# The routing ahead of a mixture of experts: the first expert turn's rows by products with one-hot matrices, its table later

## The chip, the cores and the metric

The kernel runs on one core of one Trainium2 chip. The metric is the device time in microseconds (us), as a median over runs. Everything is computed in float32.

## The reference

Two blocks of a model work on 512 tokens of 1024 features. The change is in the last stage of the second block, a mixture of experts. Cut to it:

```
group  = argmax of 4 group logits per token          # one group of 8 experts
top2   = the two best of the group's 8 expert logits # 1024 (token, choice) pairs
h      = rmsnorm(x) * gain + shift
y      = for each pair: silu(h @ w_gate[e]) * (h @ w_up[e]) @ w_down[e]
out    = rmsnorm(x + gate * (w1 * y1 + w2 * y2))
```

There are 32 experts; each has three matrices, 1024 x 512, 1024 x 512 and 512 x 1024, in float32 (2 MB each).

## The kernel before

The stage runs in 16 *turns*, and each turn works on two experts, 2n and 2n+1, with 64 row places each (`SUBROWS`): 128 rows in all. An expert with more than 64 rows gets further places in extra turns, which run only where they are wanted (`over_turns`). Ahead of the turns, `w_o_part` adds the output projection to x and makes the router's logits, and `route_part` does the routing:

- PE turns x to token-major form, in eight halves of four transposes (`turn_x(i)` in `route_part`, L3653). ACT scales each half to a row half in `tok_rows` (L3684) and puts the plain copy back in x (L3687). SP stores the four row tiles to `h_rows` in DRAM (L3638).
- DVE finds group and experts in some 20 small operations. `X` is the one-hot of each of the two choices over 32 experts, `M` their sum (L3750). Products of M with a triangular matrix and with ones give each row's *rank* within its expert (L3660, L3662).
- From rank, expert and the count of over-full experts DVE works out a slot, then the turn and the position in it (L3756 to L3774), then `numbers` (L3776) and the one-hot `one_pos` (L3780). Eight products on PE (L3668) turn these into `table`: which token and which pair stand in each place of each turn. Eight more products (L3673) give the weights of the last turn's rows.
- POOL gathers the rows of a turn from `h_rows` by `table` (L3901), and stores a turn's results to `y_rows` (L3938). A blank scatter (L4097) is sent ahead of the first.

Then the turns. PE transposes the gathered rows (`turn_x(pe, n)`, L3947); ACT (and for turn 0 DVE, L4017) applies gain and shift (L4008); PE multiplies by `w_gate` and `w_upe` (`both_experts`, L3959); ACT takes silu (L4023), DVE multiplies (L4030), PE transposes (L3979), DVE copies (L4036), PE multiplies by `w_downe` (L3959 too) and DVE scales the rows (L4042). The down product of turn n-1 stands on PE after the turn of x for n+1.

The weights come through nine slots of 2 MB. SP sends slots 0 to 7 early, slot 8 after the row stores. `send_quarters` then refills slots 0 to 7 in quarters of 512 KB (L3873): a quarter waits until two of the eight steps of the first or second turn's product have used it. From load 17 on, whole slots are sent (L3852), the first when the down product of turn 0 is done. Before the first quarter stands

```
            sp.wait_ge(gathered[0], 16)
```

Each engine runs its instructions in the order in which they are written; semaphores order the engines. The order is written out by hand: `route.tensor`, `route.vector` and so on, then the loop over turns.

Of the kernel before, what the change touches and what calls it, by code (L numbers as in the profile page):

```python
# [3592 lines left out]
Routing = collections.namedtuple("Routing", "sync gpsimd tensor scalar vector slot_weight_mm counted")  # L3593


def route_part(k, out, x, r_root, experts, weights, table, h_dram, work, at_rows, gather, y_blank, last_token, slot_weight):

# [4 lines left out]
    off = [work]  # L3602

    def buf(*dims):
        n = int(np.prod(dims))
        off[0] += n
        assert off[0] <= 6144
        x = k.at(off[0] - n, n)
# [5 lines left out]
    L, tie, one_g, ex, pg = buf(4, 36), buf(4, 8), buf(4, 4), buf(4, 4), buf(4, 1)  # L3614
    top = [buf(4, 1), buf(4, 1)]
    gmax, least, total = buf(4, 1), buf(4, 1), buf(4, 1)
    picked, masked, part = buf(4, 8), buf(4, 8), buf(4, 4, 8)
    one_e = [buf(4, 8), buf(4, 8)]
    M = buf(4, 32)
    chain, upto = buf(33), buf(33)  # L3620
    own, place, over_n, expert, slot, turn, pos, weight_in = (buf(8) for _ in range(8))
    of_over, over_from, of_turn, one_turn = buf(8, 7), buf(32), buf(8, N_COLS + 1), buf(8, N_COLS)
    one_pos = k.at(at_rows + D, D).rearrange("p (q n) -> p q n", q=8)
    X, chosen = (k.at(at_rows + a, 256).rearrange("p (i a n) -> p i a n", i=2, a=4) for a in (0, 256))
    numbers = k.at(at_rows + 512, 16 * N_COLS).rearrange("p (q t n) -> p q t n", q=8, t=2)
    of_count = k.at(40960, 224).rearrange("p (n t) -> p n t", n=32)
    late = k.at(4096, (OVER + 1) * 32).rearrange("p (o n) -> p o n", o=OVER + 1)
    halves_of_x = [x[:, 4 * (i % 2):4 * (i % 2) + 4, P * (i // 2):P * (i // 2) + P] for i in range(8)]
    x_banks = (0, 2, 3, 5)
    tok_rows = [k.at(D * tt, D) for tt in range(4)]  # L3630
    s = {n: k.sem("route_" + n) for n in ("step", "exped", "rank_in", "rank", "table_in", "table_mm", "table", "rows", "rows_out", "x_turned", "x_rows",
                                         "last_token", "weight_in", "slot_weight_mm", "counted")}
# [697 lines left out]
```

## Time and profile before

| | |
|---|---|
| median of 3 runs | 1899.35 us (1894.31 to 1899.95) |
| the profiled execution, its own time | 1896.33 us |
| its span | 1894.6 us |
| PE busy | 1722.3 us (91%) |
| DVE busy | 955.5 us |
| mean granted clock of TensorE | 0.963 |

Times in the rows are microseconds from the span's start. PE is TensorE's matmul, PEld its weight load, SPq and POOLq the issue of DMAs. A float32 product stands in the trace as two matmul records. The clock column is the granted share of full speed (1.00 is 2.4 GHz, 0.50 is 1.2 GHz).

### The profile page before, as it was taken

What the parts mean: (1) busy time and instruction counts of PE and PEld (TensorE: products, weight loads), DVE (VectorE), ACT (ScalarE), POOL (GpSimd) and SP (SyncE); (2) the same over time, 40 slices, a digit from 0 to 9 for tenths busy, and PEclk for the clock granted to TensorE, in tenths of its full rate; (3) what the DMA queues carried; (4) which work ended last, traced back from release to release, by engine and by line L of the source; (5) the groups of instructions that cost most, each with busy time, mean ns of one, the idle gap of its engine ahead of it and who ended that gap; (6) DMA issues with size and microseconds to landing.
All of it is one profiled execution on the core that took longest, in us unless ns stands there. A gap on an engine that the chain in (4) does not pass through costs nothing. (4 is left out here: it accounts for less than half of the span.)

```text
span 1894.6 us, 29840 instructions
## 1 busy us (share of the span) xinstructions
PE 1722.3 (91%) x12382; PEld 1154.4 (61%) x12382; DVE 955.5 (50%) x1605; ACT 513.3 (27%) x973; POOL 393.8 (21%) x404
## 2 busy tenths in 40 slices
PE   7999998789999999899999999899978988888877
PEld 3554487768788888788888887654443333323322
DVE  1776885556388888824588888633040001000013
ACT  4222554341354554200311112630031110110101
POOL 0000017500488887400111110100010000000000
PEclk9999999999999999899999999999979989889999
DMA  9452034204332222232584422204389999999995
GB/s 359 176 222 112 17 89 102 55 33 149 138 130 89 90 89 90 84 119 67 205 316 170 123 89 90 95 24 193 145 305 417 427 426 426 427 426 427 425 424 235
DMA packets 80537, 380.03 MB, mean 201 GB/s; under 512 B 34464, under 2 KB 37536, under 8 KB 54672
## 3 DMA queue, kind: packets, MB, share of 16 engines
q1 hardware_dynamic: 70000, 350.03, 47.7%
q0 software_dynamic: 7104, 26.68, 3.8%
q8 instruction: 100, 1.64, 0.4%
q10 hardware_dynamic: 3296, 1.38, 0.3%
q14 instruction: 37, 0.30, 0.0%
HBM read 364.09 MB, written 19.92 MB: 203 GB/s over the span
## 5 line engine op out<-in xcount | busy, mean ns | idle before, releaser
L3959 PE MATMUL psum<-mem 128*64 128x512 f32 x1504 | 355.0, 628 | 23.7 <-DMA mem<-in_w_upe 11.0
L2100 PE MATMUL psum<-mem 128*128 128x256 f32 x1232 | 270.0, 381 | 3.9 <-ACT mem L378 2.8
L3959 PEld LDWEIGHTS psum<-mem 128*64 128x64 f32 x1504 | 114.5, 144 | 244.3 <-issue 237.6
L2100 PEld LDWEIGHTS psum<-mem 128*128 128x128 f32 x1232 | 234.3, 190 | 39.7 <-ACT mem L378 3.3
L3065 PE MATMUL psum<-mem 128*128 128x256 f32 x896 | 196.9, 381 | 3.5 <-DVE mem L3246 3.0
L3065 PEld LDWEIGHTS psum<-mem 128*128 128x128 f32 x896 | 170.0, 190 | 30.3 <-issue 5.5
L2210 DVE SCALAR_TENSOR_TENSOR psum<-mem,psum 128x512 f32<-128x512 f32 x220 | 150.2, 746 | 0.0
L1681 PE MATMUL psum<-mem 128*128 128x256 f32 x594 | 132.5, 383 | 2.3 <-DMA mem<-in_w_down 1.0
L4030 DVE TENSOR_TENSOR mem<-mem,psum 128x512 f32<-128x512 f32 x16 | 11.0, 688 | 234.3 <-issue 202.0
L1681 PEld LDWEIGHTS psum<-mem 128*128 128x128 f32 x594 | 113.0, 191 | 20.8 <-issue 4.1
L2057 POOL TENSOR_TENSOR mem<-mem 128x512 f32<-128x512 f32 x88 | 111.7, 1283 | 56.7 <-ACT mem L2080 56.7
L699 PE MATMUL psum<-mem 128*128 128x512 f32 (+1 forms) x336 | 119.0, 513 | 0.0
L4042 DVE TENSOR_TENSOR mem<-psum,mem 128x512 f32<-128x512 f32 x32 | 20.6, 686 | 187.0 <-PE psum L3959 179.8
L3938 POOL DMA_INDIRECT y_rows<-mem x15 | 15.1, 1004 | 405.3 <-DVE mem L4042 368.6
L4008 ACT ACTIVATE mem<-psum,mem 128x128 f32<-128x128 f32 x124 | 45.1, 467 | 192.1 <-PE psum L3947 192.1
L699 PEld LDWEIGHTS psum<-mem 128*128 128x128 f32 x336 | 62.9, 189 | 53.4 <-issue 50.0
L3276 DVE SCALAR_TENSOR_TENSOR mem<-mem 128x512 f32<-128x512 f32 x120 | 81.4, 742 | 0.0
L566 ACT ACTIVATE mem<-mem 128x512 f32<-128x512 f32 x28 | 17.5, 630 | 208.8 <-DVE mem L1739 95.0
L3947 PE MATMUL psum<-mem 128*128 128x128 f32 x128 | 27.1, 381 | 45.5 <-DMA mem<-h_rows,mem 45.5
L4023 ACT ACTIVATE mem<-psum 128x512 f32<-128x512 f32 x16 | 9.6, 599 | 213.2 <-PE psum L3959 213.2
L2080 ACT ACTIVATE mem<-mem 128x512 f32<-128x512 f32 x88 | 60.5, 711 | 0.9 <-POOL mem L2057 0.8
L2179 DVE TENSOR_TENSOR mem<-psum,mem 128x256 f32<-128x256 f32 x66 | 27.8, 421 | 61.9 <-PE psum L2100 42.7
(447 smaller groups left out, 2613.4 us busy)
## 6 DMA issues: line engine op xcount, KB each, us to landing
mem<-in_w_upe SPq DMA_DIRECT2D x30, 2048.0 KB, 26.1
mem<-in_w_gate SPq DMA_DIRECT2D x29, 2048.0 KB, 28.3
mem<-in_w_downe SPq DMA_DIRECT2D x27, 2048.0 KB, 29.4
mem<-in_ada SPq DMA_DIRECT2D x32, 1024.0 KB, 6.9
mem<-in_w_up SPq DMA_DIRECT2D x22, 1024.0 KB, 4.9
mem<-in_ada POOLq DMA_DIRECT2D x16, 1024.0 KB, 7.0
mem<-in_w_in_g SPq DMA_DIRECT2D x12, 1024.0 KB, 5.0
mem<-in_w_down SPq DMA_DIRECT2D x16, 704.0 KB, 4.2
```

The lines of the kernel that those rows point to most:

```text
L699: last = pe.matmul(k.bank[b][:, 0:n1 - n0], w[:, kt], h[:, kt, n0:n1], start=kt == 0, stop=kt == KD - 1)
L1681: ins = pe.matmul(self.bank(bank), w[:, i], rhs[:, i], start=first and i == 0, stop=last and i == self.N - 1, skip_group_check=True)
L2057: pool.tensor_tensor(q, q, self.term[1 - row], ADD).then_inc(self.joined, 1)
L2080: act.activation(self.term[1 - row], self.window(m, row, i), ACT.Copy, scale=self.tap_weight(m, row, i)).then_inc(self.own, 1)
L2100: ins = pe.matmul(bank, w[:, i], rhs[:, i], start=first and i == 0, stop=last and i == self.N - 1, skip_group_check=True)
L2179: dve.tensor_tensor(self.place(m, row, half), four(bank), four(kept[m % 2]), ADD).then_inc(done, 1)
L2210: dve.scalar_tensor_tensor(out=a, in0=self.window(m, row, i), scalar=self.tap_weight(m, row, i), in1=base, op0=MUL, op1=ADD).then_inc(self ...
L3065: ins = pe.matmul(self.bank(bank), w[:, i], rhs[:, i], start=first and i == 0, stop=last and i == self.N - 1, skip_group_check=True)
L3276: ins = dve.scalar_tensor_tensor(out=self.conv[:, ct], in0=src, scalar=w, in1=self.conv[:, ct], op0=MUL, op1=ADD)
L3947: last = pe.transpose(k.bank[kt // 4][:, P * (kt % 4):P * (kt % 4) + P], rows[n % 2][:, P * kt:P * kt + P], k.c("ident"))
L3959: last = pe.matmul(bank[halves[h], :], xs[:, kt, halves[h]], pair[h][0][:, kt, cols], start=kt == 0, stop=kt == tiles - 1, skip_group_chec ...
L4008: ins = act.activation(x[:, kt], k.bank[kt // 4][:, P * (kt % 4):P * (kt % 4) + P], ACT.Identity, bias=shift(kt), scale=gain(kt))
```

## The change

The rows of turn 0 are no longer gathered. DVE makes `sel[0][a]`, a one-hot matrix for each of the four token tiles, by comparing the rank of the tokens of experts 0 and 1 with the numbers 0 to 63; PE multiplies `tok_rows[a]` with it, 32 products that add up in two banks, which gives x of turn 0 already turned. `sel[1][a]` does the same for experts 2 and 3, and four products with the token numbers give the row indices of turn 1's gather (`index_mm`, after the gate product of turn 0). The table of turns 0 to 15 is made from the rank alone (`one_own`, `table_mm`, after turn 0's up product). Rows past the 64th of an expert are placed by the old calculation, which moves behind turn 0's x (`places`), and their table comes after turn 1's up product (`over_mm`). The last turn's weights ride along as two further columns of `numbers`. M is made directly from the sum of the two choices, three sums replace part of the rank's products, and all of x is turned ahead of the rank. The blank scatter waits for the new table.

```diff
     def gpsimd(pool):
         pool.wait_ge(s["rows_out"], 64)
+        pool.wait_ge(x_turned, 1)
         pool.memset(y_blank[0], 0.0).then_inc(y_blank[1], 1)
-        pool.wait_ge(s["table"], 3)
-        gather(pool, 0)
+        pool.wait_ge(s["table"], 1)
         gather(pool, 1)
...
         pe.wait_ge(s["rank_in"], 1)
         m = M.rearrange("p a n -> p (a n)")
-        pe.matmul(k.bank[1][:, 0:128], k.c("before"), m, start=True, stop=False, skip_group_check=True)
-        for t in range(1, 5):
-            last = pe.matmul(k.bank[1][:, 32 * t:160], k.c("ones"), m[:, 0:160 - 32 * t], start=False, stop=t == 4, skip_group_check=True)
-        last.then_inc(s["rank"], 1)
-        for i in range(5, 8):
-            turn_x(i)
+        pe.matmul(ranks[:, 0:128], k.c("before"), m, start=True, stop=False, skip_group_check=True)
+        pe.matmul(ranks[:, 32:64], k.c("ones"), m[:, 0:32], start=False, stop=False, skip_group_check=True)
+        pe.wait_ge(s["rank_in"], 3)
+        pe.matmul(ranks[:, 64:160], k.c("ones"), sums[:, 0:3].rearrange("p a n -> p (a n)"), start=False, stop=True,
+                  skip_group_check=True).then_inc(s["rank"], 1)
+        pe.wait_ge(s["x_rows"], 5)
+        for a in range(4):
+            pe.wait_ge(s["rows"], a + 1)
+            pe.wait_ge(s["selected"], a + 1)
+            for kt in range(KD):
+                last = pe.matmul(k.bank[kt // 4][:, P * (kt % 4):P * (kt % 4) + P], tok_rows[a][:, P * kt:P * kt + P], sel[0][a],
+                                 start=a == 0 and kt % 4 == 0, stop=a == 3, skip_group_check=True)
+                if a == 3 and kt == 3:
+                    last.then_inc(s["half_turned"], 1)
+        last.then_inc(x_turned, 1)
+        pe.wait_ge(s["x_rows"], 8)
+
+    def index_mm(pe):
+        pe.wait_ge(s["selected"], 8)
+        for a in range(4):
+            last = pe.matmul(indices, sel[1][a], k.c("slot_value", 2 * a + 1, 1), start=a == 0, stop=a == 3, skip_group_check=True)
+        last.then_inc(s["index_mm"], 1)
+
+    def table_mm(pe):
+        pe.wait_ge(s["table_in"], 4)
         for q in range(8):
-            pe.wait_ge(s["table_in"], 1 + q // 4 + 1)
-            last = pe.matmul(k.bank[1][:, 256:256 + 2 * N_COLS], one_pos[:, q], numbers[:, q].rearrange("p t n -> p (t n)"), start=q == 0, stop=q == 7,
-                             skip_group_check=True)
+            last = pe.matmul(found, one_own[:, q].rearrange("p h n -> p (h n)"), numbers[:, q], start=q == 0, stop=q == 7, skip_group_check=True)
         last.then_inc(s["table_mm"], 1)
-        pe.wait_ge(s["weight_in"], 1)
+
+    def over_mm(pe):
+        pe.wait_ge(s["over_in"], 2)
         for q in range(8):
-            last = pe.matmul(k.bank[7][:, 0:1], one_pos[:, q], weight_in[:, q:q + 1], start=q == 0, stop=q == 7, skip_group_check=True)
-        last.then_inc(s["slot_weight_mm"], 1)
-        pe.wait_ge(s["last_token"], 1)
-        pe.wait_ge(s["x_rows"], 8)
+            last = pe.matmul(over_found, one_pos[:, q], over_numbers[:, q], start=q == 0, stop=q == 7, skip_group_check=True)
+        last.then_inc(s["over_mm"], 1)
...
+        step(dve, dve.tensor_tensor(either, one_e[0], one_e[1], ADD))
+        dve.tensor_tensor(M.rearrange("p a (g e) -> p a g e", g=4), of_group, either.rearrange("p a (g e) -> p a g e", g=1).broadcast_to([P, 4, 4, 8]),
+                          MUL).then_inc(s["rank_in"], 1)
+        dve.wait_ge(s["rank_in"], 1)
+        step(dve, dve.tensor_tensor(sums[:, 0:4:3], M[:, 0:4:2], M[:, 1:4:2], ADD))
+        dve.tensor_tensor(sums[:, 1], sums[:, 0], M[:, 2], ADD).then_inc(s["rank_in"], 1)
+        dve.tensor_tensor(sums[:, 2], sums[:, 0], sums[:, 3], ADD).then_inc(s["rank_in"], 1)
         for i in range(2):
             of_expert = one_e[i].rearrange("p a (g e) -> p a g e", g=1).broadcast_to([P, 4, 4, 8])
-            step(dve.tensor_tensor(X[:, i].rearrange("p a (g e) -> p a g e", g=4), of_group, of_expert, MUL), wait=i == 1)
-        dve.tensor_tensor(M, X[:, 0], X[:, 1], ADD).then_inc(s["rank_in"], 1)
-        step(dve.tensor_tensor(chosen, X, all_pairs(iota), MUL))
-        step(dve.tensor_reduce(per_pair(expert), chosen, AX, ADD))
+            step(dve, dve.tensor_tensor(X[:, i].rearrange("p a (g e) -> p a g e", g=4), of_group, of_expert, MUL), wait=False)
+        step(dve, dve.tensor_scalar(far, M[:, :, 0:4], -FAR, FAR, MUL, ADD), wait=False)
+        step(dve, dve.tensor_tensor(ex, L[:, :, 0:4], over(gmax, 4), SUB), wait=False)
+        step(dve, dve.tensor_tensor(top[1], top[1], top[0], SUB))
 
         dve.wait_ge(s["rank"], 1)
-        rank = k.bank[1][:, 0:128].rearrange("p (i a n) -> p i a n", i=1, a=4).broadcast_to([P, 2, 4, 32])
-        step(dve.tensor_tensor(chosen, X, rank, MUL), wait=False)
...
-        value = k.c("slot_value", 0, 16).rearrange("p (q t n) -> p q t n", q=8, t=2, n=1).broadcast_to([P, 8, 2, N_COLS])
-        dve.tensor_tensor(numbers, one_turn.rearrange("p q (t n) -> p q t n", t=1).broadcast_to([P, 8, 2, N_COLS]), value,
-                          MUL).then_inc(s["table_in"], 1)
+        rank = ranks[:, 0:128].rearrange("p (a n) -> p a n", a=4)
+        step(dve, dve.tensor_tensor(R, far, rank[:, :, 0:4], ADD))
+        for n in range(2):
+            for a in range(4):
+                dve.tensor_tensor(sel[n][a].rearrange("p (h n) -> p h n", h=2), every(k.c("iota", 0, SUBROWS), 2), each(R[:, a, 2 * n:2 * n + 2], SUBROWS),
+                                  ALU.is_equal).then_inc(s["selected"], 1)
+        step(dve, dve.tensor_tensor(chosen, X, ranks[:, 0:128].rearrange("p (i a n) -> p i a n", i=1, a=4).broadcast_to([P, 2, 4, 32]), MUL), wait=False)
+        step(dve, dve.tensor_tensor(of_count, each(ranks[:, 128:160], 7), every(k.c("over_at", 0, 7), 32), ALU.is_gt))
+        step(dve, dve.tensor_reduce(per_pair(own), chosen, AX, ADD))
+        value = k.c("slot_value", 0, 16).rearrange("p (q t n) -> p q t n", q=8, t=2, n=1).broadcast_to([P, 8, 2, 32])
+        dve.tensor_tensor(numbers[:, :, 0:64].rearrange("p q (t n) -> p q t n", t=2),
+                          X.rearrange("p i a (t n) -> p (i a) t n", t=1).broadcast_to([P, 8, 2, 32]), value, MUL).then_inc(s["table_in"], 1)
...
+        dve.tensor_tensor(numbers[:, :, 64:66].rearrange("p (c t) n -> p c t n", c=2), X[:, :, :, N_EXP - 2:N_EXP], of_pair, MUL).then_inc(s["table_in"], 1)
...
+    def index(dve):
+        dve.wait_ge(s["index_mm"], 1)
+        dve.tensor_scalar(table[:, 1:2, 1], indices, BLANK, float(SEQ - 1), ADD, ALU.min).then_inc(s["table"], 1)
+
+    def places(dve):
+        dve.wait_ge(s["rows_out"], 64)
         for half in range(2):
             q = slice(4 * half, 4 * half + 4)
-            dve.tensor_tensor(one_pos[:, q], every(k.c("iota", 0, P), 4), each(pos[:, q], P), ALU.is_equal).then_inc(s["table_in"], 1)
+            of_own = own[:, q].rearrange("p (q h n) -> p q h n", h=1, n=1).broadcast_to([P, 4, 2, SUBROWS])
+            dve.tensor_tensor(one_own[:, q], k.c("iota", 0, SUBROWS).rearrange("p (q h n) -> p q h n", q=1, h=1).broadcast_to([P, 4, 2, SUBROWS]), of_own,
+                              ALU.is_equal).then_inc(s["table_in"], 1)
...
     def act_part(act, n):
-        act.wait_ge(s["x_turned"], n + 1)
         if n:
+            act.wait_ge(x_turned, n + 1)
             act.wait_ge(up_mm, n)
+        else:
+            act.wait_ge(half_turned, 1)
         for kt in range(KD if n else 4):
...
             route.sync(sp)
-            sp.wait_ge(gathered[0], 16)
             experts.send_quarters(sp)
...
             pool.wait_ge(zero, 1)
+            pool.wait_ge(table_done, 7)
             pool.indirect_dma_start(y_dram, bass.IndirectOffsetOnAxis(table[:, LAST, 0:1].bitcast(U32), 0), y[1], None,
                                     bounds_check=N_PAIR - 1, oob_is_err=False).then_inc(stored[1], 16)
...
             route.tensor(pe)
-            turn_x(pe, 0)
             for n in range(N_TURN):
                 gate_up(pe, n)
+                if n == 0:
+                    route.table_mm(pe)
+                if n == 1:
+                    route.over_mm(pe)
                 if n < LAST:
...
             dve_first_part(dve)
+            route.index(dve)
+            route.places(dve)
             for n in range(N_TURN):
                 dve_hidden(dve, n)
+                if n == 0:
+                    route.table(dve)
+                if n == 1:
+                    route.over(dve)
                 if 0 < n < LAST:
                     dve_rows_out(dve, n - 1)
```

PE, from the last product of the output projection's root to turn 0. Before (L3653 transposes of x, L3660 and L3662 rank, L3668 table, L3673 weights, L3947 turn of gathered rows, L3959 expert products):

```order
L2534 MATMUL psum<-mem 128x4
L3653 MATMUL psum<-mem 128x128 x20
L3660 MATMUL psum<-mem 128x128
L3662 MATMUL psum<-mem 128x128
L3662 MATMUL psum<-mem 128x96
L3662 MATMUL psum<-mem 128x64
L3662 MATMUL psum<-mem 128x32
L3653 MATMUL psum<-mem 128x128 x12
L3668 MATMUL psum<-mem 128x48 x8
L3673 MATMUL psum<-mem 128x1 x8
L3947 MATMUL psum<-mem 128x128 x8
L3959 MATMUL psum<-mem 64x512 x32
```

The same place on PE with the change (L3668 transposes of x, L3672 to L3675 rank, L3682 selection, L4025 expert products, L3692 index, L3698 table, L4013 turn of gathered rows):

```order
L2534 MATMUL psum<-mem 128x4
L3668 MATMUL psum<-mem 128x128 x32
L3672 MATMUL psum<-mem 128x128
L3673 MATMUL psum<-mem 128x32
L3675 MATMUL psum<-mem 128x96
L3682 MATMUL psum<-mem 128x128 x32
L4025 MATMUL psum<-mem 64x512 x16
L3692 MATMUL psum<-mem 128x1 x4
L4025 MATMUL psum<-mem 64x512 x16
L3698 MATMUL psum<-mem 128x66 x8
L4013 MATMUL psum<-mem 128x128 x8
```

The table's eight products moved from ahead of turn 0 to behind its up product, four index products now stand between gate and up, the transposes of gathered rows ahead of turn 0 went, and 32 products took their place.

DVE, from the end of the choice of experts on. Before (L3749 X, L3750 M, L3751 and L3752 expert number, L3756 on: the rank used):

```order
L3744 TENSOR_TENSOR mem<-mem 128x4
L3749 TENSOR_TENSOR mem<-mem 128x128 x2
L3750 TENSOR_TENSOR mem<-mem 128x128
L3751 TENSOR_TENSOR mem<-mem 128x256
L3752 TENSOR_REDUCE mem<-mem 128x8
L3756 TENSOR_TENSOR mem<-mem,psum 128x256
```

The same place on DVE with the change (L3770 M, L3773 to L3775 sums, L3778 X, L3779 far, L3780 ex, L3787 the rank used, L3790 the eight matrices sel):

```order
L3769 TENSOR_TENSOR mem<-mem 128x32
L3770 TENSOR_TENSOR mem<-mem 128x128
L3773 TENSOR_TENSOR mem<-mem 128x2x32
L3774 TENSOR_TENSOR mem<-mem 128x32
L3775 TENSOR_TENSOR mem<-mem 128x32
L3778 TENSOR_TENSOR mem<-mem 128x128 x2
L3779 TENSOR_SCALAR mem<-mem 128x16
L3780 TENSOR_TENSOR mem<-mem 128x16
L3782 TENSOR_TENSOR mem<-mem 128x4
L3787 TENSOR_TENSOR mem<-mem,psum 128x16
L3790 TENSOR_TENSOR mem<-mem 128x128 x8
```

M stands ahead of X, three small sums are new, and what first uses the rank is one addition and the eight comparisons.

## Rows read from the trace of the kernel before

**Rows 1.** The page: DMA's busy tenths in 40 slices of the span.
```profile
DMA  9452034204332222232584422204389999999995
```
**Rows 2.** Windows: us, busy PE, PEld, DVE, ACT, POOL, clock, DMA share, GB/s.
```profile
1373.40:1397.10 23.70, 13.46 (x88) 11.23 (x88) 15.12 (x61) 11.35 (x21) 0.95 (x1) 0.79 0.93 354
1397.10:1409.20 12.10, 10.21 (x38) 6.63 (x40) 3.94 (x15) 2.79 (x5) 4.11 (x4) 0.56 0.46 146
1409.20:1451.00 41.80, 39.38 (x184) 14.48 (x182) 3.95 (x6) 7.00 (x18) 0.98 (x1) 0.96 1.01 397
1451.00:1850.00 399.00, 334.93 (x1450) 123.61 (x1448) 36.72 (x63) 45.55 (x117) 27.27 (x28) 0.91 1.01 426
```
**Rows 3.** The chain that ended last: start, us, what.
```profile
1397.27 4.52 DMA mem<-h_rows,mem
...
1404.51 15.62 PE psum L3959 x64
1420.13 1.04 PE psum L3947 x8
...
1421.55 2.56 ACT mem L4008 x7
1424.15 15.67 PE psum L3959 x64
...
1440.85 7.04 PE psum L3959 x32
```
**Rows 4.** Timeline of DVE: start, us, line, operation, idle before and releaser.
```profile
1382.80 0.49 DVE L3749 TENSOR_TENSOR mem<-mem 128x128 f32<-128x128 f32 x2
1383.32 0.29 DVE L3750 TENSOR_TENSOR mem<-mem 128x128 f32<-128x128 f32 x1
...
1385.88 0.42 DVE L3756 TENSOR_TENSOR mem<-mem,psum 128x256 f32<-128x256 f32 x1 [1.47 <-PE psum L3662]
...
1391.63 1.29 DVE L3780 TENSOR_TENSOR mem<-mem 128x512 f32<-128x512 f32 x2
```
**Rows 5.** Timeline of PE, the same columns.
```profile
1383.67 0.55 PE L3660 MATMUL psum<-mem 128*128 128x128 f32 x2 [3.81 <-DVE mem L3750]
...
1385.58 2.38 PE L3653 MATMUL psum<-mem 128*128 128x128 f32 x12
1392.37 3.65 PE L3668 MATMUL psum<-mem 128*128 128x48 f32 x16 [4.41 <-DVE mem L3780]
```
**Rows 6.** Timeline of ACT.
```profile
1386.71 0.69 ACT L3684 ACTIVATE mem<-psum,mem 128x512 f32<-128x512 f32 x1 [3.30 <-PE psum L3653]
```
**Rows 7.** Timeline of SP's DMA issues.
```profile
1379.75 10.13 SPq L3638 DMA_DIRECT2D h_rows<-mem  x4
...
1408.17 0.33 SPq L3873 DMA_DIRECT2D mem<-in_w_downe  x1
...
1440.23 0.43 SPq L3873 DMA_DIRECT2D mem<-in_w_gate  x1
1447.91 0.33 SPq L3852 DMA_DIRECT2D mem<-in_w_gate  x1
```
**Rows 8.** Windows of 1 us, columns as in rows 2.
```profile
1384.00:1385.00 1.00, 1.00 (x8) 1.00 (x6) 0.41 (x1) 0.00 (x0) 0.00 (x0) 0.50 0.95 279
...
1387.00:1388.00 1.00, 0.96 (x7) 0.72 (x5) 0.93 (x6) 1.00 (x3) 0.00 (x0) 0.81 0.99 406
```
**Rows 9.** Groups by form: 128x128 products elsewhere in the kernel.
```profile
L753 PE MATMUL psum<-mem 128*128 128x128 f32 x96 | 12.3, 278 | 3.2 <-ACT mem L865 3.2
```
**Rows 10.** DMA, 1396.5 to 1409.5, 1397 to 1402, 1449 to 1452: us to landing.
```profile
q0 software_dynamic: 576, 1.72, 40.7%
...
mem<-h_rows,mem POOLq DMA_INDIRECT x2, 5.8
...
y_rows<-mem POOLq DMA_INDIRECT x1, 11.4
mem<-h_rows,mem POOLq DMA_INDIRECT x1, 15.6
```

More of the change, by code:

```diff
@@ L3590, in _, with route_part, shaped @@
                 dve.tensor_tensor(mix[:, m], gate_a[:, m], gate_b[:, m], ADD).then_inc(s["mix"], 1)
-Routing = collections.namedtuple("Routing", "sync gpsimd tensor scalar vector slot_weight_mm counted")
-def route_part(k, out, x, r_root, experts, weights, table, h_dram, work, at_rows, gather, y_blank, last_token, slot_weight):
+Routing = collections.namedtuple("Routing", "sync gpsimd tensor scalar vector index_mm table_mm over_mm index places table over counted table_done")
+FAR = 4096.0
+def route_part(k, out, x, r_root, experts, weights, table, h_dram, work, at_rows, at_places, gather, y_blank, last_token, slot_weight, x_turned):
     nc = k.nc
[L3602 to L3608, printed above, removed]
+    at = {"early": work, "late": work + D_EXP}
+    ends = {"early": work + D_EXP, "late": 6144}
+    def shaped(x, dims):
         if len(dims) == 2:
@@ L3613, in buf @@
         return x
[L3614 to L3622, printed above, removed]
@@ new lines, in route_part @@
+    part = buf("early", 4, 4, 8)
+    tie, picked, masked = buf("early", 4, 8), buf("early", 4, 8), buf("early", 4, 8)
+    one_g, ex, pg = buf("early", 4, 4), buf("early", 4, 4), buf("early", 4, 1)
+    top = [buf("early", 4, 1), buf("early", 4, 1)]
+    gmax, least, total = buf("early", 4, 1), buf("early", 4, 1), buf("early", 4, 1)
+    chain, upto, own, over_n = buf("early", 33), buf("early", 33), buf("early", 8), buf("early", 8)
+    M, one_e, either = buf("late", 4, 32), [buf("late", 4, 8), buf("late", 4, 8)], buf("late", 4, 8)
@@ new lines, in route_part @@
+    numbers, over_numbers, pos = buf("late", 8, 66), buf("late", 8, 2 * OVER_TURNS), buf("late", 8)
+    one_turn = k.at(at_L, 8 * OVER_TURNS).rearrange("p (q n) -> p q n", q=8)
+    place, expert, slot, turn = (k.at(at_L + 8 * OVER_TURNS + 8 * i, 8) for i in range(4))
+    of_over = k.at(at_part, 56).rearrange("p (q n) -> p q n", q=8)
+    of_turn = k.at(at_part + 56, 8 * (OVER_TURNS + 1)).rearrange("p (q n) -> p q n", q=8)
+    X, chosen = (k.at(4096 + o, 256).rearrange("p (i a n) -> p i a n", i=2, a=4) for o in (0, 256))
@@ L3723, in first_max @@
[L3723 to L3726 removed]
+            step(dve, dve.scalar_tensor_tensor(out=t, in0=t, scalar=-100.0, in1=ids_n, op0=MUL, op1=ADD))
+            step(dve, dve.tensor_reduce(least, t, AX, ALU.min))
+            step(dve, dve.tensor_tensor(one, t, over(least, n), ALU.is_equal))
+        dve.wait_ge(out.logits[1], 1)
+        step(dve, dve.memset(chain[:, 0:1], 31.0), wait=False)
@@ new lines, in places @@
+        step(dve, dve.tensor_tensor(place, place, expert, ADD))
+        step(dve, dve.scalar_tensor_tensor(out=slot, in0=place, scalar=float(SUBROWS), in1=own, op0=MUL, op1=ADD))
+        step(dve, dve.tensor_tensor(of_turn, each(slot, OVER_TURNS + 1), every(k.c("turn_at", N_TURN, OVER_TURNS + 1), 8), ALU.is_ge))
+        step(dve, dve.tensor_reduce(turn.rearrange("p (q o) -> p q o", o=1), of_turn[:, :, 1:OVER_TURNS + 1], AX, ADD), wait=False)
+        step(dve, dve.tensor_tensor(one_turn, of_turn[:, :, 0:OVER_TURNS], of_turn[:, :, 1:OVER_TURNS + 1], SUB))
```

204 lines of the change are left out of this document (111 added, 93 removed).

## Prediction

> **What bounds the kernel now.** I read the windows of the last stage first. From 1451 to 1850 us the 16 DMA engines are full: share 1.01, 426 GB/s, while PE works 334.93 of 399 us [rows 2]; the page's DMA line shows the same nines to the end [rows 1]. The expert weights are a fixed number of bytes, so this stretch gets no shorter; the stage can end earlier only if the stream saturates earlier. Next the windows ahead of it: 354 GB/s from 1373.4 to 1397.1, then 146 GB/s from 1397.1 to 1409.2, then 397 [rows 2]. That is 8.39 + 1.77 + 16.6 MB, 26.75 MB in all in 77.6 us. At the 410 GB/s of a full queue of quarter loads (an estimate from the 397 of a window whose first us was still filling) they are 65.3 us, so some 12.3 us of DMA time is lost before 1451. That is the ceiling for any earlier start.
>
> Why is it lost? SP has nine slots to fill; the next load goes out at 1408.17, when the first eighth of the first turn's weights has been used [rows 7]. The chain says what that waits for: gather of the rows (4.52 us), turning them, the gate product from 1404.51 [rows 3]. Gather 0 waits for the table, and that for DVE's chain from the rank at 1385.88 to 1392.92 [rows 4] and for the table's product, 3.65 us on PE [rows 5].
>
> **The change, part by part.** (1) *To the rank.* Before, M stands behind two products for X (0.49 us) and is ready at 1383.61 [rows 4]. Now one 128x32 sum (about 0.2, an estimate from the spacing of small operations) and M; ex, moved behind, gives 0.1 back. M: about 1383.2. PE then has 6 matmul records instead of 10 (a float32 product is two records, as the x16 for 8 products shows [rows 5]), but waits for three small sums (about 0.65 us) before its last two. Before, the rank came 2.2 us after PE's start at 1383.67 [rows 4, 5]; now about 1384.75. In that time DVE does X, far, ex and top, so R starts about 1384.85 and the first sel matrix (0.25 us, as one L3749 [rows 4]) is there at 1385.3. PE starts at 1385.4. The other seven come every 0.25 us, faster than PE uses them.
>
> (2) *PE no longer stops ACT.* All eight halves of x are turned before the rank. ACT's 3.30 us stop [rows 6] goes, so the fourth row tile is ready near 1386.0 (PE needs it after 1391), and SP, which ended the four row stores at 1389.88 [rows 7], comes to the last slot's load about 3.3 us earlier. This alone moves no end: the nine slots are full by about 1395 instead of 1397, and the stream still waits for a free quarter.
>
> (3) *The first x by products.* 32 products, 64 records. At the half clock a record of full weights costs 3.65/16 = 0.228 us [rows 5]; at the full clock 12.3/96 = 0.128 us [rows 9]. Bounds: 8.2 and 14.6 us. The granted clock fell to 0.50 by 1384 after 3.81 us without work, and came back to 1.0 during 1387 to 1388, under the products and transposes of the 4 us ahead [rows 5, 8]. The new stream starts with less idle time before it and has no gaps, so I take 12 records slow and 52 at 0.13: 2.7 + 6.8 = 9.5 us. PE ends at 1394.9; ACT's half of x is ready by then, since the first half bank is released eight records earlier. The gate product starts at 1395.0 instead of 1404.51 [rows 3]: **9.5 us earlier**.
>
> The Trainium skill, "TensorE: Matmul & The Clock Gate" (Part 4, PE-mode transpose), says that transposes do not count as busy work for the clock. By that rule the transposes left between 1380 and 1383 would not hold the clock and the selection would begin slow, as I have assumed; the trace cannot separate this, as products and transposes stand together in that stretch.
>
> (4) *The first quarter.* It needs eight records of 128x512. Before: 3.66 us, to 1408.17, at the low clock [rows 3, 7]. Now PE arrives warm: 8 x 7.04/32 = 1.76 us [rows 3]. SP's next load is issued at 1396.8, **11.4 us earlier**. SP's removed wait for gather 0 costs nothing either way, since this semaphore comes later.
>
> (5) *What falls into the full stretch.* The four POOL transfers took 1.72 MB between 1396.5 and 1409.5 [rows 10], while the queue was nearly empty. Gather 0 (128 rows of 4 KB, 0.52 MB) goes; the others, 1.2 MB, now run beside the stream. Turns 2 and 3 now fetch clamped rows too: up to 0.5 MB more. 1.7 MB at 410 GB/s is **4.1 us back**. DMA's side of the sum: -11.4 + 4.1 = -7.3.
>
> (6) *PE's side.* The quarters cover two turns; the next load, at 1447.91 [rows 7], waits for the first down product, 43.4 us after the first gate product. Now: 43.4 - 1.5 (turn 0's 15.62 us become 64 x 0.22 = 14.1 [rows 3]) + 1.05 (index, 8 records) + 2.1 (table) + 2.1 (over), each record 0.13 = 47.15. From 1395.0 it is 1442.15, 5.8 us earlier. Before, quarters were still moving at 1447.91: the last was issued at 1440.23 [rows 7], and the 16.8 MB of two turns take 41 us from the first at 1408.17, to about 1451. So a gap of 0 to 1.5 us may open there. I take 0.6: **-6.7**.
>
> DVE's tail, now behind the index: places is about 30 operations, 8.5 us, from gate start + 8.3 to + 17; it holds up hid of turn 0 by 1.7 us, and PE wants that only after turn_x(1), at + 18.4. The cover is 1 us; without it PE would wait the difference. The weights and numbers lie beside the selection, where DVE otherwise has nothing to do. Table(0) delays hid_t of turn 0 to + 21.5; the down product that reads it is 20 us later. POOL: the blank scatter and gather 2 are queued behind the table, leave at about + 20, and are wanted at + 39.
>
> (7) *Gather 1* is the new wait. It leaves POOL when gate (7.05), index (1.05) and POOL's start (1.1) are over, at + 9.2; PE wants it at + 17.3 (14.1 + 1.05 + 2.1). On an idle queue it lands in 5.8 us, behind a scatter and among whole-slot loads in 15.6, the scatter alone in 11.4 [rows 10]: bounds 5.8 and 15.6. Here there is no scatter ahead, and the loads beside it are quarters in 4 KB rows; I take 7, so it costs nothing, with 1 us to spare.
>
> The Trainium skill, "DMA: Bandwidth & Descriptors" (Queues, rings and completion order), says that an engine takes turns between queues by packet. By that rule a short gather waits for a few weight packets only, near my 7; the trace's 15.6 shows that long packets make these turns dear.
>
> **Sum.** -6.7 on the profiled 1896.33 us is 1889.6. The median of the runs shown, 1899.35, is 3.0 above the profiled one, so the forecast on it is **1892.6**.
>
> **Rivals.** *Full clock throughout* (0.10): the selection takes 8.2 us, another 1.3 us gained, -8: 1891.3. For it: PE's idle stretches ahead of the selection get shorter than the 3.81 us after which the clock fell. Against: the transposes before it still come in short bursts.
>
> *Half clock throughout* (0.12): selection 14.6 us, gate at 1400.1 and a slow first quarter: -4.4 + 4.1, about 0: 1899. For it: from 1392 on, PE's short products ran wholly at 0.228 a record [rows 5]. Against: [rows 8].
>
> *Gather 1 is late* (0.10), the one on the other side: over 8.1 us after its issue every further us delays turn 1, and with it the load that waits for the first down product. At 15.6 this is 7.5 us: -5.8 + 7.5 = +1.7, 1901. It decides from 14 us on. For: the stream is full when it leaves. Against: no scatter ahead.
>
> *The transfers are hidden anyway* (0.06): the stream starts early but another wait, hid or the turn of x, starves it at once: -1, 1898. Against: 12.3 us of DMA time lost in [rows 2].
>
> *As forecast* (0.62): -4.5 to -8.5, 1891 to 1895.
>
> **How the numbers follow.** About 0.3%, 5.7 us, is what a measurement of this kernel can tell from no change; the three runs lie 5.6 us apart. Of the main case two thirds are beyond 5.7 us, 0.41, and of the full-clock case all: 0.51 faster. The rest of the main case, half clock, hidden transfers and most late gathers are within 0.3%: 0.43. A gather later than any row shows, or one that also holds turn 2, is the 0.06 slower. The range takes the cases from -11 (nearly all lost DMA time) to the half clock: 1887 to 1899.
>
> **What would show it.** The selection: 64 records in 8.2 to 14.6 us, from about 1385.4, then the gate product at 1394 to 1396. First quarter load 11 us earlier, near 1397. 400 GB/s from 1399 on, without a hole near 1418 to 1421 (between turns 0 and 1) or 1443 to 1446. PE's wait for gather 1: none; if it is several us, part 7 is wrong. A gate product after 1398 makes part 3 wrong. If both stand and the time is unchanged, then part 5 or 6 is.

## The result, and the profile after

The changed kernel took 1884.42 us (median of 6 runs, 1881.1 to 1886.4), the kernel before 1895.35 us (median of 6, 1890.9 to 1899.95): ratio 0.9941, interval 0.9929 to 0.9954. That is 10.9 us faster, or 0.6%; the forecast was 6.7 us faster, 1892.6.

The profiled spans, 1894.6 and 1879.3 us, can't be subtracted as they stand: the part of the program ahead of the change ended 6.2 us sooner in this one execution of the changed kernel (another of the same kernel, below, ended it at 1377.80). I count from a moment that both share, **t0**, when DVE's L2565 begins, ahead of the routing. It was 1377.42 us before and is

```profile
1371.25 0.18 DVE L2565 RECIPROCAL mem<-psum 128x4 f32<-128x4 f32 x1 [1.37 <-PE psum L2534]
```

From t0 to the end of the span are 517.18 us before and 508.05 after: 9.1 less.

PE after (start, us, line, operation, idle before and its releaser); the answer to [rows 3, 5]:

```profile
1376.97 0.49 PE L3672 MATMUL psum<-mem 128*128 128x128 f32 x2
...
1378.83 7.38 PE L3682 MATMUL psum<-mem 128*128 128x128 f32 x64 [0.81 <-DVE mem L3790]
1386.14 7.10 PE L4025 MATMUL psum<-mem 128*64 128x512 f32 x32
1393.17 1.05 PE L3692 MATMUL psum<-mem 128*128 128x1 f32 x8
1394.15 7.10 PE L4025 MATMUL psum<-mem 128*64 128x512 f32 x32
1401.18 2.00 PE L3698 MATMUL psum<-mem 128*128 128x66 f32 x16
1403.41 1.09 PE L4013 MATMUL psum<-mem 128*128 128x128 f32 x8 [0.22 <-DMA mem<-h_rows,mem]
...
1407.50 13.99 PE L4025 MATMUL psum<-mem 128*64 128x512 f32 x64 [2.51 <-ACT mem L4078]
```

The selection (L3682) runs 7.38 us, 0.115 a record, and the gate product begins at t0 + 14.9; before it was t0 + 27.1, so it is 12.2 us earlier. SP's issues, the answer to [rows 7]:

```profile
1373.58 6.72 SPq L3653 DMA_DIRECT2D h_rows<-mem  x4
1380.34 0.84 SPq L3917 DMA_DIRECT2D mem<-in_w_downe  x1
1388.12 0.33 SPq L3938 DMA_DIRECT2D mem<-in_w_downe  x1
...
1421.89 0.87 SPq L3938 DMA_DIRECT2D mem<-in_w_gate  x1
1431.35 0.33 SPq L3917 DMA_DIRECT2D mem<-in_w_gate  x1
```

The first quarter goes out at t0 + 16.9 instead of 30.75, 13.9 us earlier; the first whole load at t0 + 60.1 instead of 70.5, 10.4 earlier. Windows (columns as in rows 2), the answer to [rows 2, 8]:

```profile
1373.40:1396.00 22.60, 20.50 (x135) 13.19 (x135) 12.21 (x53) 12.03 (x23) 1.65 (x2) 1.00 0.99 376
1396.00:1409.20 13.20, 10.47 (x62) 5.37 (x60) 9.50 (x38) 2.90 (x8) 2.83 (x3) 1.00 1.03 410
1409.20:1451.00 41.80, 37.34 (x185) 14.40 (x182) 3.50 (x7) 4.10 (x10) 2.03 (x2) 0.99 1.03 418
1451.00:1840.00 389.00, 322.24 (x1409) 120.83 (x1409) 36.09 (x62) 47.03 (x119) 26.24 (x26) 0.93 1.01 425
...
1378.00:1379.00 1.00, 0.20 (x2) 0.20 (x2) 0.93 (x6) 1.00 (x3) 0.00 (x0) 1.00 0.65 197
```

The hole of 146 GB/s is gone, and the granted clock (third column from the end) stays at its upper level, 2.4 GHz, through the routing and turn 0, where before it was at 0.79 and 0.56 of it in the first two windows. By such windows the DMA engines moved 33.4 MB from t0 - 4 to t0 + 80, against 29.6 before: 3.8 MB more, which at 426 GB/s is 9.0 us, as much as the span lost. Both then go on at 425 to 426 GB/s. That the two figures agree within 0.1 us is in part luck, as other traces below show.

GpSimd after, and the transfers' time from issue to landing (1393 to 1412 us), the answer to [rows 10]:

```profile
1395.30 1.28 POOL L3966 DMA_INDIRECT mem<-h_rows,mem  x1 [7.71 <-DVE mem L3812]
1404.82 1.23 POOL L4167 DMA_INDIRECT y_rows<-mem  x1 [8.23 <-PE psum L4013]
1406.35 1.02 POOL L3966 DMA_INDIRECT mem<-h_rows,mem  x1 [0.30 <-issue]
...
q0 software_dynamic: 314, 1.04, 13.6%
...
mem<-h_rows,mem POOLq DMA_INDIRECT x2, 8.3
y_rows<-mem POOLq DMA_INDIRECT x1, 7.5
```

Gather 1 left 9.2 us after the gate product's start and made PE wait 0.22 us.

### The profile page after: what moved, and what is told of

The parts are those of the page before. It is cut to its first block and busy times, and to the rows that moved or that the text cites. A ratio compares the mean times of both kernels' runs of the same rounds, so it can differ in the third digit from the quotient of the medians.

```text
span 1879.3 us, 29988 instructions
## 1 busy us (share of the span) xinstructions
PE 1715.1 (91%) x12442; PEld 1153.8 (61%) x12442; DVE 960.0 (51%) x1631; ACT 512.9 (27%) x973; POOL 393.1 (21%) x403
## 5 line engine op out<-in xcount | busy, mean ns | idle before, releaser
L4025 PE MATMUL psum<-mem 128*64 128x512 f32 x1504 | 351.1, 622 | 37.6 <-DMA mem<-in_w_upe 19.5
L4025 PEld LDWEIGHTS psum<-mem 128*64 128x64 f32 x1504 | 115.6, 143 | 252.0 <-issue 245.6
L1582 PE MATMUL psum<-mem 128*128 128x512 f32 x128 | 56.9, 597 | 1.8 <-PEq L3508 1.8
L2179 DVE TENSOR_TENSOR mem<-psum,mem 128x256 f32<-128x256 f32 x66 | 27.7, 420 | 60.1 <-PE psum L2100 42.7
## 6 DMA issues: line engine op xcount, KB each, us to landing
mem<-in_w_downe SPq DMA_DIRECT2D x27, 2048.0 KB, 30.9
```

The source lines that it names most:

```text
L1582: last = pe.matmul(self.banks[m % len(self.banks)][:, :], w, self.rhs[:, kt], start=i == 0, stop=i == n - 1)
L2179: dve.tensor_tensor(self.place(m, row, half), four(bank), four(kept[m % 2]), ADD).then_inc(done, 1)
L4025: last = pe.matmul(bank[halves[h], :], xs[:, kt, halves[h]], pair[h][0][:, kt, cols], start=kt == 0, stop=kt == tiles - 1, skip_group_chec ...
```

## Experiments

All runs are of whole kernels. What each is worth is read twice: as the ratio of its runs to those of the kernel before on the same chip, and from t0 in its trace. "L" lines are those of each experiment's own kernel.

**The changed kernel again**, with nothing edited, as the base of the others.

> The changed kernel once more, as the base for the others of this call. The earlier runs gave a ratio of 0.9941 to the kernel before (about 11 us). From the two traces the last stage alone, counted from the reciprocal that ends the output projection, accounts for 9.1 us (517.2 us before, 508.1 us after). If the rest was chance between executions, the ratio comes out near 0.995 to 0.9955; if the change also does something ahead of the stage, it stays at 0.994.

Ratio 0.9948 (0.993 to 0.9967), medians 1886.89 and 1897.25; first quarter at t0 + 16.9, span from t0 507.70. The first trace was no exception, in its early part or in its span. The kernel before has a median of 1897.25 over 33 runs here, so the 1899.35 on which the forecast was put was the high side of its spread.

**The kernel before with PE kept busy.** Is the gain the clock's alone? Products that nobody reads are put into PE's idle stretches: 7 ahead of the rank, 10 ahead of the table, 3 and 5 behind it.

```diff
+        def busy(count):
+            for _ in range(count):
+                pe.matmul(k.bank[4][:, 0:512], k.c("ident"), k.c("quarter", 0, 512), start=True, stop=True, skip_group_check=True)
+
         for i in range(5):
             turn_x(i)
+        busy(7)
         pe.wait_ge(s["rank_in"], 1)
...
+        busy(10)
         for q in range(8):
...
+        busy(3)
         pe.wait_ge(s["weight_in"], 1)
...
+        busy(5)
```

> The kernel before, with products that nobody reads (constants by constants, into a bank that is free) put on PE where it has nothing to do: 7 ahead of the rank, 10 ahead of the table, 3 ahead of the last turn's weights, 5 while the first gather runs. This holds the granted clock up and changes nothing else. Theory A (the gain is the earlier first x, found without the table and the gather): most of it stays out. The table's 16 records go from 3.65 to about 2.1 us, the turn of x from 1.96 to 1.04 us and the first quarter from 3.66 to 1.76 us, so the first quarter load comes some 4 us earlier and the time falls by about 4 us, less than half of the change's. Theory B (the gain is mostly the clock, and the products with one-hot matrices only keep PE busy): 8 us or more. If the clock is worth nothing because the transfers have slack: 0.

Ratio 1.0019 (1.0004 to 1.0034). One such product took 0.87 us (two records of 0.44), twice what I had counted, so they stood in front of ready work: the first quarter went out at t0 + 33.4, 2.65 us later than before, and the span from t0 grew by 4.6. The granted clock was 1.00 in the windows from t0 - 4 to t0 + 32, but the delay hides what that is worth, so I repeated it with fewer.

**The same with 3, 5, 1 and 3 products.**

> The kernel before with unread products on PE, now 3 ahead of the rank, 5 ahead of the table, 1 ahead of the last turn's weights and 3 while the first gather runs; each is two records of 512 columns, 0.86 us at the full clock, so none stands in front of work that is ready. (With 7, 10, 3 and 5 they did: the ninth slot's load went out 0.7 us later and the first quarter 2.65 us later, counted from the reciprocal that ends the output projection.) The measure is the time from that reciprocal to the end of the span: 517.2 us in the kernel before, 508.1 and 507.7 us in two executions of the changed one. Theory A (the clock is a part only): the clock holds, table, turn of x and first quarter gain up to 1.5 + 0.9 + 1.9 us, the end comes 3 to 4.5 us earlier, 513 to 514 us. Theory B (the clock is most of the gain): 510 us or less.

Ratio 0.9996 (0.9981 to 1.0011); first quarter at t0 + 27.9 (2.85 us earlier than before), span from t0 515.8 (-1.4). Its PE:

```profile
1391.79 1.99 PE L3674 MATMUL psum<-mem 128*128 128x48 f32 x16 [0.98 <-DVE mem L3788]
...
1395.65 1.95 PE L3680 MATMUL psum<-mem 128*128 128x1 f32 x16 [0.95 <-DVE mem L3805]
1397.46 4.52 PE L3658 MATMUL psum<-mem 128*128 128x512 f32 x6
```

The table takes 1.99 us where it took 3.65 [rows 5]. In the wait for the gather the clock fell nevertheless (the last row: six records in 4.52 us instead of 2.6), and these products held up the turn of x. The better clock thus gave the kernel before 2.9 us at the first quarter. The last products ran over by 1.9 us; without that it would have given some 4.8 (an estimate, no run shows it). By it some 9 of the 13.9 us are not to be had so. At the end little of it arrives: the ratio tells no gain from none, and the 515.8 misses the 513 to 514 expected.

**The changed kernel with the gate product held up** by 12 unread products behind the selection. If the earlier resume of the weights is the gain, a later resume must give it back one for one.

```diff
         last.then_inc(x_turned, 1)
         pe.wait_ge(s["x_rows"], 8)
+        for _ in range(12):
+            pe.matmul(k.bank[4][:, 0:512], k.c("ident"), k.c("quarter", 0, 512), start=True, stop=True, skip_group_check=True)
```

> The changed kernel with 12 unread products (about 5.2 us at the full clock) on PE between the selection and turn 0's gate product. Theory A (the stream of weights is the bound and each us of its later start is paid): the ninth slot is still loading when the first quarter is freed (it landed 11.1 us after its issue at 1380.34, 3.3 us after the first quarter load's issue at 1388.12), so some 2 to 3 us of the delay are hidden and 2.5 to 4 us are paid. Rival (the transfers are hidden, something else ends the stage): 0 to 1 us. Rival (fully exposed): 5.2 us.

Ratio 1.0007 (0.9989 to 1.0024): the whole gain is gone. The products took 10.47 us, not the 5.2 that I had counted; the first quarter went out 10.3 us later than in the changed kernel and the span from t0 grew by 9.7 (517.56 against a mean of 507.9), 0.94 us for each. Of the slack of 2 to 3 us that I had allowed for, at most 0.6 us is there. The first quarter is still 3.6 us ahead of the kernel before here, and yet the time is the same: the transfers that now fall into the full stretch take that much back.

```profile
1384.72 7.38 PE L3682 MATMUL psum<-mem 128*128 128x128 f32 x64 [0.80 <-DVE mem L3792]
1391.94 10.47 PE L3689 MATMUL psum<-mem 128*128 128x512 f32 x24
1402.34 7.11 PE L4027 MATMUL psum<-mem 128*64 128x512 f32 x32
```

**The changed kernel with three halves of x turned behind the rank again**, as before. It opens an idle stretch ahead of the rank: is that where the clock would fall, and the selection run slow?

```diff
-        for i in range(8):
+        def turn(i):
...
+        for i in range(5):
+            turn(i)
...
+        for i in range(5, 8):
+            turn(i)
         pe.wait_ge(s["x_rows"], 5)
```

> The changed kernel with the last three halves of x turned behind the rank again, as in the kernel before. It undoes one part of the change. If that part only frees ACT, the fourth row tile comes about 3 us later, still before PE's last eight products need it, and the transposes add about 1.6 us ahead of the selection: 0 to 1.5 us slower. If it is what held the clock (it fell in the kernel before after 3.81 us without work at this place), the clock falls again here, the selection takes 9 to 11 instead of 7.4 us, and with the slack of 2 to 3 us the time rises by 1 to 4 us.

Ratio 0.996 (0.9945 to 0.9975); first quarter 1.7 us later than in the changed kernel, span from t0 1.9 longer.

```profile
1381.42 0.79 PE L3675 MATMUL psum<-mem 128*128 128x128 f32 x2 [3.27 <-DVE mem L3775]
1382.01 0.47 PE L3676 MATMUL psum<-mem 128*128 128x32 f32 x2
1382.30 0.72 PE L3678 MATMUL psum<-mem 128*128 128x96 f32 x2
1382.81 2.44 PE L3668 MATMUL psum<-mem 128*128 128x128 f32 x12
1385.09 7.31 PE L3687 MATMUL psum<-mem 128*128 128x128 f32 x64
```

After 3.27 us without work the rank's records are slow, as in the kernel before. The clock comes back in the last of the twelve transposes (0.50 from 1383 to 1384, 0.61 from 1384 to 1385, then 1.00), and all of the selection is at the upper level. The early turn of x is what keeps the rank's records fast (0.49 us for the first two, against 0.79) and saves 1.7 us in all; it isn't what keeps the selection fast.

**The changed kernel with index and table ahead of the gate product.** The first x still comes from products, but the table is back where it was.

```diff
-        if n == 0:
-            route.index_mm(pe)
...
             route.tensor(pe)
+            route.index_mm(pe)
+            route.table_mm(pe)
             for n in range(N_TURN):
                 gate_up(pe, n)
-                if n == 0:
-                    route.table_mm(pe)
```

> The changed kernel with the index and table products on PE ahead of turn 0's gate product instead of behind its gate and up products. It undoes the part of the change that puts the table later; the first x still comes from the one-hot matrices. PE then waits for DVE's first half of x, the index and the two one-hot matrices of own (1.36 + 0.16 + 1.28 us) and does 24 records (3 us). Theory A: the first quarter load goes out 4 to 5 us later than in the changed kernel (16.9 us after the reciprocal), and the end comes 3.5 to 5 us later, 511.5 to 513 us. Rival (the order of the table is worth nothing): 508 us.

Ratio 0.996 (0.9943 to 0.9976), medians 1890.51 and 1897.27. The first quarter goes out 6.4 us later than in the changed kernel, the span from t0 is 513.50, 5.6 longer; 4 to 5 and 3.5 to 5 were expected. By medians (1886.89 for the changed kernel) it is 3.6 longer, and the intervals of the two ratios overlap, so the size at the end is less sure than that at the first quarter.

```profile
1382.77 7.38 PE L3682 MATMUL psum<-mem 128*128 128x128 f32 x64 [0.80 <-DVE mem L3790]
1389.99 0.95 PE L3692 MATMUL psum<-mem 128*128 128x1 f32 x8
1392.88 2.05 PE L3698 MATMUL psum<-mem 128*128 128x66 f32 x16 [1.94 <-DVE mem L3819]
1394.86 15.58 PE L4025 MATMUL psum<-mem 128*64 128x512 f32 x64
```

The wait for DVE of 1.94 us in front of the table is followed by a gate product that starts at half the clock. So of the 13.9 us at the first quarter about 6.4 come from the table's new place, and 7.5 from the rest, above all (no run splits it) the products in place of the gather.

**Which empty places fetch rows.** A place of a turn without a token can point past the last row, and is then skipped, or be clamped to row 511, and is then fetched. The changed kernel clamps turns 1 to 3. One kernel clamps none, the other all. Only what empty places fetch changes; a place that fetches nothing keeps what its tile held, and its result is never stored. One of the lines of the first kernel:

```diff
-        dve.tensor_scalar(table[:, 1:2, 1], indices, BLANK, float(SEQ - 1), ADD, ALU.min).then_inc(s["table"], 1)
+        dve.tensor_scalar(table[:, 1:2, 1], indices, BLANK, None, ADD).then_inc(s["table"], 1)
```

> The changed kernel with the row indices of turns 1 to 3 not limited to 511, so that the empty places of those gathers fetch nothing (in turns 1 to 3 such places keep an earlier row, whose result is never stored). It takes 3 x about 0.25 MB out of the full stretch. Theory A (bytes moved into the full stretch are paid at the stream's rate): 1.5 to 2 us less, 506 us from the reciprocal to the end. Rival (small gathers fit in gaps of the stream): 0.

> The changed kernel with the row indices of all 16 turns limited to 511, so that every gather fetches 128 rows. That adds about 12 x 0.25 MB = 3 MB to the full stretch. Theory A: 3 MB at 425 GB/s, 7 us more, about 515 us from the reciprocal to the end. Rival (gathers fit in gaps): 0 to 1 us.

None clamped: ratio 0.9941 (0.9922 to 0.9959), span from t0 505.78, 2.1 us less than the changed kernel's mean. All clamped: 0.9992 (0.9979 to 1.0006), 514.81, 6.9 more. The queue of these transfers over the span (packets, MB, share), in the changed kernel, with none and with all clamped:

```profile
q0 software_dynamic: 6960, 26.66, 3.8%
```
```profile
q0 software_dynamic: 6960, 25.97, 3.7%
```
```profile
q0 software_dynamic: 6960, 30.02, 4.2%
```

0.69 MB less and 3.36 MB more, at 425 GB/s 1.6 and 7.9 us, where the spans show 2.1 and 6.9. Once the stream is full a byte costs about its time. Ahead of that it doesn't: the kernel before with its first two gathers unclamped, further below, moves 0.32 MB less in all and has a ratio of 0.9992.

**The ninth slot's load ahead of the row stores**, in the changed kernel.

```diff
     def sync(sp):
+        experts.send(sp, 8, 9)
         for tt in range(4):
...
-        experts.send(sp, 8, 9)
```

> The changed kernel with the ninth slot's load issued ahead of the four stores of the row tiles instead of behind them. The trace of the changed kernel shows DMA at 211 GB/s for the 2 us from 1378 to 1380, while SP waits for the last row tile. Theory A (any gap of the DMA engines in the stage is paid, wherever it lies before the stream is full): 0.8 to 1 us less. Rival (the first free quarter decides, what lies ahead of it is free): 0.

Ratio 0.995 (0.9932 to 0.9968), span from t0 508.53, 0.7 more: nothing gained. My main theory (0.8 to 1 us less) missed. The rival was right: the first free quarter decides, and a gap of the DMA engines ahead of it costs nothing.

**Three small parts of the change done alone in the kernel before**: no clamp for turns 0 and 1; all of x turned ahead of the rank; no wait for gather 0 on SP.

```diff
-        for i in range(5):
+        for i in range(8):
             turn_x(i)
...
-        for i in range(5, 8):
-            turn_x(i)
```

> The kernel before with the row indices of turns 0 and 1 not limited to 511: two gathers that fetch about 0.25 MB less each. The same edit in the changed kernel, for turns 1 to 3, took 2.1 us off the time from the reciprocal to the end (505.8 against 507.7 and 508.1). Theory A (bytes count only in the stretch where the stream is full): in the kernel before these gathers run while the DMA engines are nearly idle, so only the first gather's landing can come earlier: 0 to 0.7 us less, 516.5 to 517.2 us. Rival (fewer bytes always help): 1.2 us less or more.

> The kernel before with all eight halves of x turned ahead of the rank: this part of the change alone. Theory A: ACT is freed 3 us earlier and the ninth slot's load goes out about 3 us earlier, but the first quarter still waits for the table and the gather; it may come up to 1 us earlier where the clock stays up. 0 to 1 us less, 516 to 517 us. Rival (the earlier stores and ninth slot are worth their 3 us): 514 us.

> The kernel before without SP's wait for the first gather ahead of the quarter loads. The first quarter is freed 6 us after that gather has landed, so the wait never ends last: 0, 517.2 us. Rival (the wait keeps something back that the change sets free): over 1 us.

Ratios 0.9992 (0.998 to 1.0004), 1.0001 (0.9985 to 1.0016) and 0.9988 (0.9974 to 1.0001); first quarter at t0 + 30.9, 29.9 and 31.1, before 30.75. With x turned early the ninth slot's load left at t0 + 9.1 instead of 12.5 and bought nothing.

These three also show how far single traces of such a kernel lie apart. Their spans from t0 are 519.5, 519.9 and 522.2 us, where 516 to 517.2 were expected; before's is 517.2. The bytes moved by t0 + 80 (28.9, 30.0 and 29.3 MB, before's 29.6) don't explain it: the second is 0.4 MB ahead of before and ends 2.7 us later. Part of it is in the last products of the program, here those of the third:

```profile
1871.99 3.75 PE L4143 MATMUL psum<-mem 128*128 128x512 f32 x4 [2.80 <-issue]
1875.53 3.20 PE L4149 MATMUL psum<-mem 128*128 128x512 f32 x4
1878.56 1.88 PE L4143 MATMUL psum<-mem 128*128 128x512 f32 x4
```

The granted clock is 0.89 from 1869 to 1872, the wait ahead of them, and 0.50 from 1872 to 1876, and the first two groups take 3.1 us more than in the changed kernel:

```profile
1857.94 1.96 PE L4219 MATMUL psum<-mem 128*128 128x512 f32 x4 [1.19 <-issue]
1859.74 1.88 PE L4225 MATMUL psum<-mem 128*128 128x512 f32 x4
```

## Why the prediction came out wrong

The step that failed is part 3, the selection's length and clock: with the rank's 0.4 us it put the first quarter 2.5 us too late. Beside it, the 1899.35 us that the sum was put on lay 4.0 us too high.

**The mechanism was right.** The stage is bound by the weight stream; the first x by products lets it resume earlier, and the end follows: 0.94 us for each with the gate product held up, 0.88 with the table ahead, 1.1 with x turned later, each from one trace (three traces that resume alike lie 0.8 us apart). No hole opened between turns. The rivals of a late gather and of transfers hidden anyway are out: PE waited 0.22 us for gather 1, and bytes in the full stretch cost their time (the two clamp runs).

**To the rank (1):** the selection began at t0 + 7.6, put at 8.0. Right.

**The ninth slot (2):** its load left 3.4 us earlier, put at 3.3, and is worth nothing, as two runs show.

**The selection (3) is the step that failed.** I took 12 records at half clock and 52 at 0.13, 9.5 us, inside bounds of 8.2 and 14.6. It took 7.38, below the lower one. Two errors. The price of a full-speed record, 0.128 us from [rows 9], was that of a group in another stage, whose 96 records run in eight bursts of 12; here 64 run in one, and it is 7.38/64 = 0.115. That is about 0.9 us. And the clock never fell, about 1.2 us: the rival "full clock throughout", to which I gave 0.10, is what happened. What I held for half clock, the table's 0.228 a record [rows 5], came behind 4.41 us of waiting for DVE, a wait that the change itself takes away; with PE kept busy ahead of it the same table ran in 1.99 us. With 0.4 us from the rank and 2.3 from here (it spans 7.31 us from its start to the gate product's) the gate product was 12.2 us earlier, not 9.5.

The rule of the Trainium skill that I had set beside this step, "TensorE: Matmul & The Clock Gate" (Part 4, PE-mode transpose), would have let the clock fall ahead of the selection. The trace doesn't agree: from 1371.07 to 1376.89 PE ran transposes of x alone, and the window of that stretch has the upper level. The kernel with x turned later shows it more sharply. There, too, 5.9 us pass from the first transpose to the rank (1375.53 to 1381.42, here 1371.07 to 1376.97), but without the last twelve transposes, and the rank's first two records take 0.79 us. They take 0.49 in the six traces that I compared with all of x turned early. So here the transposes did hold the clock.

```profile
1371.00:1376.00 5.00, 4.00 (x31) 3.04 (x30) 4.11 (x21) 4.20 (x8) 0.00 (x0) 1.00 1.01 433
```

**The first quarter (4)** followed the gate product's start by 1.98 us, put at 1.8; so it was 13.9 us earlier, not 11.4.

**The bytes (5):** 4.1 us were to be given back; from 13.9 at the first quarter to the 9.1 and 9.5 of the end (two traces) 4.4 to 4.8 are. Right within 0.7.

**PE's side (6):** the first down product was put at 47.15 us behind the gate product and came at 45.2 (1431.35 - 1386.14). I had taken only turn 0's products to the upper clock; turn 1's ran in 13.99 us too, where they took 15.67 [rows 3]. That isn't fixed by the change: with the ninth slot's load first they took 15.68, and the end moved by 0.7 us only. The gap of 0.6 us that I allowed is not in the windows.

**Gather 1 (7):** put at 7 us, took 8.1 (bounds 5.8 and 15.6). The cover was as small as stated, and just held. Of my two reasons, no scatter ahead and quarters beside it, the traces point to the second: gather 2, issued 1.5 us behind the blank scatter but among quarter loads still, landed in 8.5 us, while gathers behind a scatter among whole-slot loads took 14.6 to 15.6 in later turns. The blank scatter moves little, though, so its weight isn't ruled out. A packet of the weights held about 3.6 KB among the quarters (6.49 MB in 1783) and 14.6 KB among whole slots (8.31 MB in 570, 1460 to 1480 us before).

**The sum:** -13.9 + 4.1 = -9.8 by the measured first quarter, against -9.1 and -9.5 from t0. So of the 2.6 us by which the profiles (9.3 on the mean) beat the forecast of 6.7, the first quarter (the clock and the record's price 2.1, the rank 0.4) gave 2.5 and the gap that did not open 0.6, while 0.5 more was given back than put. The rest of the miss, from 1892.6 down to 1884.4, is mostly in what it was put on: the median of 3 runs, 1899.35, was 4.0 us above that of 6, and by medians the gain is 10.9 rather than 9.3. Even the full-clock rival's 1891.3 was too high. The range has a slip of its own: 11 us below 1899.35 is 1888, not 1887. Counted from 1895.35, the forecast would have been 1888.7, 4.2 us too high. The 1.6 us between the gain by profiles, 9.3, and that by medians, 10.9, lie within the spread of single traces: before's own is the shortest of the four that resume at t0 + 30 to 31. The mean of those four from t0 is 519.7 us, that of the three of the changed kernel that resume at 16.9 without a change in bytes (the profile after, its repeat, the ninth slot first) is 508.1: 11.6 less. Of these, 8.7 are there when the last turn's down product starts; 1.6 come in the wait between it and the last products, and 1.3 in and behind those, some of it at the low clock. Why that wait was shorter in the changed kernel isn't shown, and chance isn't excluded.

**A version that may be better still** is the changed kernel with no clamp: bytes for 1.6 us fewer, 2.1 us less from t0 (505.78). By medians it isn't told apart from the changed kernel (1885.39 on one chip, 5 runs; 1886.89 on another; the intervals of the ratios overlap).

## What to carry to other kernels

When a stage ends in a long stretch of full DMA, count the bytes moved by a fixed point ahead of it: 3.8 MB at 426 GB/s, 9.0 us, foretell most of the difference here. They don't foretell what happens behind that stretch, where single traces of much the same kernel lay up to 5 us apart. Before a product is priced at the low clock, ask what idle stretch made the clock fall in the trace, and whether the change removes that stretch: half the cost seen may go with it. Take a record's price from a group that runs in one stretch as long as yours: short bursts cost 0.128 us a record, one stream 0.115. And put a forecast on as many runs as there are; three runs 5.6 us apart moved this one by 4 us.

## What the runs showed of the hardware

- How long PE had been idle doesn't alone decide the clock. After 3.27 us without work its records ran below the upper level, and the selection that began 3.67 us later ran at it (the kernel with x turned later); gaps of 0.41 us between groups of four transposes, and one of 0.81 us, left it at the top (the changed kernel). With 1.94 us of waiting behind the index products the table still ran fast (2.05 us for 16 records), and the gate product behind it began at half clock, as this window of the kernel with the table ahead of the gate product shows:

```profile
1395.00:1396.00 1.00, 1.00 (x4) 0.38 (x6) 0.86 (x5) 0.00 (x0) 0.00 (x0) 0.50 0.57 184
```

- Ahead of the program's last products waits of 2.17, 2.62 and 2.80 us (table first, all clamped, no wait for gather 0) were followed by four records in 3.62 to 3.75 us, one of 2.72 us (the kernel before) by the same four in 1.96.
- In the second kernel with PE kept busy, six 128x512 records took 4.52 us in the gather's wait, right behind the 16 single-column records of the weights. PE had no idle time between, and yet the granted clock was 0.66 from 1398 to 1399 and 0.50 for the 2 us after.
- On full DMA engines gathers of 128 rows landed in 7.8 to 8.5 us beside quarter loads, one of them behind the blank scatter; [rows 10] have 15.6 us for one behind a scatter among whole-slot loads.
- At the upper level a float32 record of 512 columns lasts 0.59 us (the median) with 64 weight columns as with 128, but their spacing differs. With 128 they follow each other every 0.436 us (10.47 us for 24). With 64, where the records of two experts alternate and fill different halves of the output's 128 partitions, it is 0.22 us (7.10 for 32).
